# Prompt attention of a hybrid layer: the product of probabilities and values turned, split in two parts, and scaled afterwards

## The reference

```
s = einsum('bqhd,bkhd->bhqk', q_blk, k) * (FOX_HD ** -0.5)
s = s + (cq[..., :, None] - ckT[..., None, :])      # c: running sum of log f
s = where(kpos <= qpos, s, -inf)
p = softmax(s, axis=-1)
o = einsum('bqhk,bkhd->bqhd', p, v)
```

## Time and profile before

| | us |
|---|---|
| median of three runs | 1702.04 |
| lowest, highest | 1701.9, 1707.56 |
| span of the profiled execution | 1703.1 |
| PE busy in it | 1601.3 |
| DVE, ACT, POOL busy | 819.5, 663.1, 236.0 |
| fox's rounds, 484 to 736 us | 252 |

### The profile page before, as it was taken

The page is one execution under the profiler, slowest core; times in us unless marked ns, Lnnn a source line. Parts: engine busy times, 40 slices in busy tenths (PEclk is TensorE's granted clock), DMA queues, the critical chain, the costliest instruction groups (busy, mean ns, idle before and its releaser), DMA issues. The chain is left out here.

```text
span 1703.1 us, 25703 instructions
## 1 busy us (share of the span) xinstructions
PE 1601.3 (94%) x9847; PEld 1464.5 (86%) x9847; DVE 819.5 (48%) x1362; ACT 663.1 (39%) x1117; POOL 236.0 (14%) x292
## 2 busy tenths in 40 slices
PE   7999999999999999999999999999998599999980
PEld 7988898889989898999999999999787488888760
DVE  3433463353033433313032323233647799999975
ACT  5422241222254554522112111112212488888866
POOL 1000120013011111130000000000000254443220
PEclk9999999999999999999999999999998699999995
DMA  6111231125211112062325124111432899999736
GB/s 183 40 38 38 73 112 49 36 66 167 78 48 41 68 44 79 19 188 79 126 62 179 46 66 143 38 38 67 162 132 81 278 265 273 326 300 290 190 60 230
DMA packets 154225, 204.34 MB, mean 120 GB/s; under 512 B 14723, under 2 KB 121235, under 8 KB 154104
## 3 DMA queue, kind: packets, MB, share of 16 engines
q1 hardware_dynamic: 135224, 140.82, 26.3%
q0 software_dynamic: 18880, 61.89, 13.1%
HBM read 152.34 MB, written 50.34 MB: 119 GB/s over the span
## 5 line engine op out<-in xcount | busy, mean ns | idle before, releaser
L380 PE MATMUL ps<-xh,slab_hi 128*128 128x384 f32 (+1 forms) x504 | 171.8, 341 | 1.4 <-DVE slab_lo L732 1.4
L380 PE MATMUL ps<-xh,slab_lo 128*128 128x384 f32 (+1 forms) x504 | 165.1, 328 | 0.0
L380 PE MATMUL ps<-xl,slab_hi 128*128 128x384 f32 (+1 forms) x504 | 165.0, 327 | 0.0
L1899 PE MATMUL ps<-xh,slab_lo 128*128 128x384 f32 (+1 forms) x384 | 125.2, 326 | 0.0
L1899 PE MATMUL ps<-xh,slab_hi 128*128 128x384 f32 (+1 forms) x384 | 125.1, 326 | 0.0
L1899 PE MATMUL ps<-xl,slab_hi 128*128 128x384 f32 (+1 forms) x384 | 125.1, 326 | 0.0
L2100 DVE TENSOR_TENSOR gt_sg<-ps,gt_sg 128x384 f32<-128x384 f32 (+1 forms) x48 | 25.7, 536 | 186.5 <-PE ps L1899 186.3
L380 PEld LDWEIGHTS ps<-xh,slab_hi 128*128 128x128 f32 x504 | 95.0, 188 | 15.4 <-issue 13.6
L2869 PE MATMUL ps<-mo_hi_gu,mo_xh 128*128 128x512 f32 x256 | 100.3, 397 | 0.9 <-ACT mo_xh L2972 0.7
L2869 PE MATMUL ps<-mo_hi_gu,mo_xl 128*128 128x512 f32 x256 | 98.9, 391 | 0.0
L2040 ACT ACTIVATE gt_sg<-ps 128x384 f32<-128x384 f32 (+1 forms) x48 | 22.7, 473 | 191.1 <-PE ps L1899 191.1
(11 more groups left out here) (500 smaller groups left out, 4219.3 us busy)
## 6 DMA issues: line engine op xcount, KB each, us to landing
slab_raw<-in_w_in SPq DMA_DIRECT2D x60, 512.0 KB, 4.2
mo_raw_g<-in_w_e_gate SPq DMA_DIRECT2D x16, 1024.0 KB
mo_raw_u<-in_w_e_up SPq DMA_DIRECT2D x16, 1024.0 KB
mo_raw_d<-in_w_e_down SPq DMA_DIRECT2D x16, 1024.0 KB
gt_oh<-oT_hi SPq DMA_DIRECT2D x3, 2176.0 KB, 7.8
gt_ol<-oT_lo SPq DMA_DIRECT2D x3, 2176.0 KB, 12.7
slab_raw<-in_w_branch SPq DMA_DIRECT2D x24, 256.0 KB, 4.6
x_dram<-slab_raw SPq DMA_DIRECT2D x9, 512.0 KB, 5.1
```

The costliest lines, as they stand in the source:

```text
L380: mm = eng.matmul(out, w[:, b, k, :], x[:, k, t0:t0 + tn], start=(k == 0 and j == 0), stop=(k == KC - 1 and j == 2), skip_group_check=True)
L1899: last = eng.matmul(out, w[:, s % 2, c, wk, :], x[:, k, t0:t0 + tn], start=(k == 0 and i == 0), stop=(k == ks[-1] and i == 2))
```

## The change

The product is turned: the values, in two fp32r parts side by side (`vhl`, 128 columns), are the stationary operand, and the transposed probabilities, also in two fp32r parts (`PT`, 256 columns), the moving one. One matmul per key tile and head gives, in PSUM bank 7, rows 0 to 63 (remainder of v) and 64 to 127 (leading part of v), each for both parts of the probabilities. ACT copies the quarter "remainder of v by leading part of P" to SBUF, DVE sums the two quarters of the upper rows, POOL adds both and multiplies by the reciprocals. Since queries lie on columns now, the reciprocals have to stand on all 64 rows: SP stores them to DRAM (`r_dram`) and loads them back broadcast (`r_all`). No transpose of the output is left. The remainder of the probabilities is a new step on DVE (`probs_low`), and PSUM banks 5 and 6 come free after it (`bank_freed`). The stores of the output move from POOL to SP, the loads of `cb` too, and `cb` has one buffer per head instead of two. Weight blocks 9 to 11 and the first gate weights are loaded between SP's other steps. `mpos`, `ident16`, `mf` and some small buffers lie elsewhere, with waits that guard them.

```diff
         @block.gpsimd
+            def finish(Q):
+                eng.wait_ge(low_ready, BASE + Q + 1)
+                eng.wait_ge(high_ready, BASE + Q + 1)
+                ch(eng.tensor_tensor(oT[:, :, :], oT[:, :, :], oT_high[:, :, :], ALU.add))
+                eng.wait_ge(r_moved, BASE + 32 * Q + 32)
+                ch(eng.tensor_tensor(oT[:, :, :], oT[:, :, :], r_all[:, :, :], ALU.mult))
...
-                eng.wait_ge(oT_lo, Q + 1)
-                store_branch(sh, eng, 1, slice(128 * p, 128 * p + 128), slice(128 * qt, 128 * qt + 128),
-                             oh[:, Q % 2, :], ol[:, Q % 2, :], o_st[Q % 2])
+                finish(Q)
         @block.sync
+            def spread_inverse(Q):
+                if Q >= 1:
+                    eng.wait_ge(r_moved, BASE + 32 * Q)
+                eng.wait_ge(rinv_done, Q + 1)
+                eng.dma_start(sh.r_dram[Q % 2].rearrange("h n -> n h"), rinv[:, Q % 2, :],
+                              allow_slow_non_contiguous=True).then_inc(r_moved, 16)
+                eng.wait_ge(r_moved, BASE + 32 * Q + 16)
+                if Q >= 1:
+                    eng.wait_ge(pool_s, scaled(Q - 1))
+                eng.dma_start(r_all[:, :, :], sh.r_dram[Q % 2].unsqueeze(0).broadcast_to([HD, 2, 128])).then_inc(r_moved, 16)
+            spread_inverse(0)
+            for Q in range(NQ):
                 p, qt = divmod(Q, 8)
+                if Q + 1 < NQ:
+                    spread_inverse(Q + 1)
+                if p < 3 and qt == 5:
+                    rows(eng, p + 1)
                 eng.wait_ge(oT_lo, Q + 1)
+                for dst, src in ((sh.oT_hi, oh), (sh.oT_lo, ol)):
+                    eng.dma_start(dst[1, 128 * p:128 * p + 128, 128 * qt:128 * qt + 128].rearrange("(h d) n -> d h n", h=2),
+                                  f32(src[:, :, :])).then_inc(o_st[Q % 2], 16)
...
             for i in range(2):
                 eng.wait_ge(o_st[i], 32 * (NQ // 2))
         @block.tensor
+        def bank_freed(eng, C):
+            if C >= 2:
+                if C - 2 in prob_of:
+                    eng.wait_ge(pt_lo, BASE + prob_of[C - 2] + 1)
+                else:
+                    eng.wait_ge(pt_out, C - 1)
...
-                eng.wait_ge(pt_out, last(chunk_no, Q, h) + 1)
+                if h == 0 and qt == 0:
+                    eng.wait_ge(v_tail, p + 1)
+                eng.wait_ge(pt_lo, BASE + last(out_no, Q, h) + 1)
                 for t in range(qt + 1):
-                    mm = eng.matmul(sh.ps[:, 7, 64 * h:64 * h + 64], PT[:, h, t, :],
-                                    v[:, t, 64 * (2 * p + h):64 * (2 * p + h) + 64],
+                    mm = eng.matmul(sh.ps[:, 7, 256 * h:256 * h + 256], vhl[:, t, h, :, :].rearrange("p s d -> p (s d)"),
+                                    PT[:, h, t, :, :].rearrange("p s n -> p (s n)"),
...
-                if Q >= 1:
-                    transpose_out(Q - 1)
         @block.scalar
+                if Q >= 1:
+                    bring_low_half(Q - 1)
+                if Q % 8 == 0:
+                    split_values(Q // 8)
                 place_unit(Q, 0)
                 place_probs(Q, 0)
                 if Q + 1 < NQ:
                     exponent(Q + 1, 0)
-                if Q >= 1:
-                    out_head(Q - 1)
                 place_unit(Q, 1)
                 place_probs(Q, 1)
...
+                if Q >= 1:
+                    out_head(Q - 1)
         @block.vector
+                if Q >= 1:
+                    sum_high_half(Q - 1)
+                if Q % 8 == 0:
+                    split_values(Q // 8)
                 if Q + 1 < NQ:
                     lowest(Q + 1, 0)
                 tail_unit(Q, 0)
                 if Q + 1 < NQ:
                     lowest(Q + 1, 1)
+                probs_low(Q, 0)
+                tail_unit(Q, 1)
+                probs_low(Q, 1)
                 if Q >= 1:
                     out_tail(Q - 1)
-                tail_unit(Q, 1)
                 tail_unit(Q, 2)
```

More of the change, by code:

```diff
@@ L1106, in keys, with scaled, rows @@
             return 512 * c, min(512, kn - 512 * c)
+        def scaled(Q):
+            return 4 + 2 * Q + 2
+        def bank_freed(eng, C):
[4 more added lines that the diff above has]
+                    eng.wait_ge(pt_out, C - 1)
+        def rows(eng, p):
+            for h in range(2):
+                if p >= 1:
+                    eng.wait_ge(s_out, last(out_no, 8 * p - 1, h) + 1)
+                eng.dma_start(cb[:, h, :],
+                              sh.c_dram[0, 2 * p + h:2 * p + h + 1, 0:SEQ].broadcast_to([128, SEQ])).then_inc(c_in[h], 16)
         @block.gpsimd
         def _(eng):
-            def rows(p):
-                if p >= 2:
-                    eng.wait_ge(s_out, last(out_no, 8 * (p - 2) + 7, 1) + 1)
-                for h in range(2):
-                    eng.dma_start(cb[:, 2 * (p % 2) + h, :],
-                                  sh.c_dram[0, 2 * p + h:2 * p + h + 1, 0:SEQ].broadcast_to([128, SEQ])).then_inc(c_in[p % 2], 16)
+            def finish(Q):
[4 more added lines that the diff above has]
+                ch(eng.tensor_tensor(oT[:, :, :], oT[:, :, :], r_all[:, :, :], ALU.mult))
             def store_keys(p):
@@ L1131, in _ @@
             ch(eng.tensor_copy(ident16[:, :], sh.ident[:, :]))
-            rows(0)
-            rows(1)
             eng.wait_ge(unit_free, V_UNITS)
@@ L1138, in _ @@
             for Q in range(NQ):
-                p, qt = divmod(Q, 8)
-                eng.wait_ge(oT_lo, Q + 1)
-                store_branch(sh, eng, 1, slice(128 * p, 128 * p + 128), slice(128 * qt, 128 * qt + 128),
-                             oh[:, Q % 2, :], ol[:, Q % 2, :], o_st[Q % 2])
-                if p < 3 and qt == 4:
-                    store_keys(p + 1)
-                if p < 2 and qt == 7:
-                    rows(p + 2)
-            for i in range(2):
-                eng.wait_ge(o_st[i], 32 * (NQ // 2))
+                finish(Q)
+                if Q < 24 and Q % 8 == 4:
+                    store_keys(Q // 8 + 1)
             eng.wait_ge(v_st, 32)
@@ new lines, in _ @@
+            for n in range(RW, 9):
+                load_block(n)
+                if n == 5:
+                    eng.wait_ge(pool_s, 4)
+                    rows(eng, 0)
+            def spread_inverse(Q):
[8 more added lines that the diff above has]
+                eng.dma_start(r_all[:, :, :], sh.r_dram[Q % 2].unsqueeze(0).broadcast_to([HD, 2, 128])).then_inc(r_moved, 16)
@@ L1164, in _ @@
+            for i in range(2):
+                eng.wait_ge(o_st[i], 32 * (NQ // 2))
         @block.tensor
@@ L1488, in lowest @@
                 p, I = Q // 8, 2 * Q + h
-                if Q % 8 == 0 and h == 0:
-                    eng.wait_ge(c_in[p % 2], 32 * (p // 2 + 1))
+                if Q % 8 == 0:
+                    eng.wait_ge(c_in[h], 16 * (p + 1))
                 if I >= 3:
@@ new lines, in split_values, with probs_low @@
+            def split_values(p):
+                eng.wait_ge(v_head, p + 1)
+                eng.tensor_tensor(vhl[:, :, :, 0, :], v[:, :, 128 * p:128 * p + 128].rearrange("p t (h d) -> p t h d", h=2),
+                                  f32(vhl[:, :, :, 1, :]), ALU.subtract).then_inc(v_tail, 1)
+            def probs_low(Q, h):
+                for c in range(n_chunk(Q)):
+                    C = chunk_no[Q, h, c]
+                    eng.wait_ge(pt_out, C + 1)
+                    nt = min(4, Q % 8 + 1 - 4 * c)
+                    eng.tensor_tensor(PT[:, h, 4 * c:4 * c + nt, 1, :],
+                                      sh.ps[:, 5 + C % 2, 0:128 * nt].rearrange("p (t n) -> p t n", t=nt),
+                                      f32(PT[:, h, 4 * c:4 * c + nt, 0, :]), ALU.subtract).then_inc(pt_lo, 1)
@@ L1542, in _ @@
                     tail_half(sh, eng, 0)
[L1543 to L1544 removed]
+                if Q + 1 < NQ:
+                    row_inverse(Q + 1)
+            sum_high_half(NQ - 1)
             out_tail(NQ - 1)
@@ L1720, in _ @@
                                  channel_multiplier=1))
+            eng.wait_ge(*sh.fox.oT_lo)
             ch(eng.memset(selh[:, :, :], 0.0))
@@ L3202, in build @@
         sh.m_head, sh.m_tail = sem("m_head"), sem("m_tail")
+        with ExitStack() as over:
+            sh.mpos, sh.ident16 = (over.enter_context(nc.sbuf_tensor(n, [128, 128], BF16)) for n in ("mpos", "ident16"))
         sh.lg = sb("lg", [128, NT, NE])
```

119 lines of the change are left out of this document (74 added, 45 removed).

## The result

The changed kernel takes **1847.77 us** (median of 4, 1846.4 to 1848.33), the kernel before 1701.97 beside it: 1.085 times as long, 95% interval 1.0836 to 1.0863. The forecast was 1693, the range 1680 to 1705. It is slower by 146 us, by rival 3, which had a chance of 0.05.

The account below looks back on a forecast made before the run. PE was taken to bound the kernel (244.49 of 252.00 us busy in these rounds). Terms: -38.0 + 20.6 + 4.7 + 4.2 - 3.0 + 2.3 = -9.2 us, from 1702.04 to 1693; range 1680 to 1705.

Parts of the forecast that it names:

- rival 3: Slower: the reciprocals' round trip through DRAM decides if landings exceed 6.15 us each; 1730 us at 7 each; chance 0.05.
- the reciprocals' two small transfers: On SP each round: store and load back, 4.4 us for both within a 7.9 us round, costing nothing.
- SP's other steps: On SP: reordered cb rows, weight blocks and stores, each a round or more before its reader, costing nothing.
- The product: On PE: 576 old instructions, 67.8 us, become 288 matmuls of 0.119 us, 34.3 us; gain 33.5 us.
- The output transposes: On PE: all 32 removed, 0.14 us each, a gain of 4.5 us.
- banks 5 and 6: PE's transposes wait for DVE's remainder of the probabilities, 1.41 to 1.68 us from five key tiles on; +20.6 us in all.
- key transposes: On PE, behind head 1's transposes at n = 3 to 5: longer waits for DVE, +4.7 us together.
- the product's: On PE: the product waits for head 1's remainders, +2.8 us, and for split values at n = 1, +1.4; together +4.2.
- The passage: Into the gates stage: a 0.58 us wait goes, but PE waits 2.9 us for the first key page; +2.3 us.
- Rival 2: Waits eat the gain: about 50 new waits each 0.2 us longer, +10, 1703 us (1698.5 to 1708); chance 0.17.
- Rivals 1 and 4: First: PE hardly held up, 1672 to 1687 us, chance 0.20. Fourth: new matmuls at 0.235 us, 1712 us, chance 0.03.
- Pool's operations: On POOL: two new operations of 256 elements, 0.5 us each (0.3 to 1.0), hidden in half a round, costing nothing.

## Why the prediction was wrong

**The step that failed** is "the reciprocals' two small transfers [...] in a sequence on SP that has a round [...] at nothing", with rival 3's condition. Two numbers were wrong, and it took both. The landing: 2.2 us for 64 KB was taken as the nearest row, though the text itself named the 256 pieces of 4 bytes and that no row shows such a landing; it is 7.3. The bound of this unknown never entered the range. And the loop: "covers two rounds, so it decides once two landings and some 3.5 us [...] exceed 15.8 us, landings of over 6.15 us each". The code lets the store of block Q + 1 go only when the load of block Q has landed, so store landing, load landing and what lies between must fit into one round of 7.9 us: 7.62 + 4.14 doesn't. Even with 8-byte landings, 3.2 and 3.3, it is at the edge. The run with the store sent twice shows this chain by itself. The right landings alone would not have mended the forecast: in a loop of two rounds, 7.3 + 3.5 (the load's median in the run with two queues) + 3.5 us is under 15.8. Nor would the right loop alone: at 2.2 us a landing it takes some 5 us of the 7.9, an estimate from 2.2 + 2.2 and the 0.6 that is left of the round of 11.76 beside 7.62 and 3.5.

**Bigger by the trip:** about 129 us of the 146. The run without transfers has it by stage (120.1 + 8.8), the one turned on TensorE is 128.6 below the change while it pays 9.6 us on PE, and 8-byte pieces alone give back 120. With it goes another term at nothing, SP's other steps: in the change DVE waits 24.9 us in 6 for the rows of `cb`, in the runs without the trip not at all.

**The product** was sized at 33.5 us. The old pace was 0.114 (65.6 / 576), not 0.118, because 67.8 us are ends less starts of overlapping matmuls; the new one is the 0.119 taken. Gain: 65.6 - 34.3 = 31.3, 2.2 too much in the forecast. **The output transposes** held PE 2.3 us, not 4.5: the 0.14 were also a duration; the distance to the next start is 0.07 on the mean. With these, -38.0 would have been -33.6.

**The new waits** came out near: banks 5 and 6 18.8 for 20.6, key transposes 9.2 for 2.2 + 4.7, the product's 3.3 inside its own rows (37.6 - 34.3) and 1.1 beside them for 4.2. All idle of PE in the rounds rose by 25.3; the terms give 20.6 + 4.7 + 0.9 - 3.0 = 23.2 without the 3.3. Not in the sum at all was that the filler pieces run slower between such waits, 3.7 us. So in the kernel turned on TensorE the rounds are -33.6 + 28.6 + 3.7 = -1.3 without its transposes, where the forecast had -11.5, and +8.3 with their 9.6; the span says +8.2. These parts are read from the same two traces as the whole, so that they add up shows only that none is missing.

**The passage**, +2.3, is +5.1 there and +17.9 in the change. The late page was foreseen (2.9 us for 3.62), the half clock behind it was not, nor, in the change, that DVE's tail of the output stands ahead of the gates unit.

**Rival 2** (waits eat the gain, 1698.5 to 1708) is nearest to what the change would be with a free trip, and still too low: the run without transfers has +5.9 in the rounds and +9.1 in the passage, which makes some 1717, an estimate without its 8 us behind the router. So the forecast gain would not have come with a free trip either. **Rivals 1 and 4** are out: PE did stand at the transposes, and the new matmuls go at 0.119. Pool's operations, 0.73 and 0.80, show no cost of their own in the rounds, as said.

Open: what the 8 us late in the run without transfers are; why the passage is 9.1 us longer there and 5.1 with the reciprocals turned on TensorE; and whether stores of other pieces than these three shapes follow size or number, or the layout in DRAM, which changed with the piece size.

## What to carry to other kernels

When a step goes through DRAM and back, count the landings that must be over before the next one may be issued, and compare them with one round of the loop; buffers don't help when the waits on the issuing queue are serial. The small store's landing went by its piece size before its bytes here: lay the small array out so that pieces are larger, or keep it on chip, and keep urgent transfers from behind such a store. What PE gains is the distance between starts, not the busy time of overlapping matmuls. And an order on an in-order queue (DVE's remainder, SP's last wait) gave 9.4 and 7 to 10 us for a few moved lines, about as much each as the whole forecast gain of 9.2.
